# Moving a mixture-of-experts block's down product into the middle of the next block's gate and up product

## The reference, cut to what matters

```
def block_ffn(args):
    xb, e = args
    return (jax.nn.silu(xb @ w_gate[e]) * (xb @ w_up[e])) @ w_down[e]

yb = lax.map(block_ffn, (xin, blk_e)).reshape(NB * MOE_BLOCK, D)
y_assign = yb[dest] * sw[:, None]
routed = jax.ops.segment_sum(y_assign, stok, num_segments=T)
```

## Time and profile before

| what | value |
|---|---|
| time, median of 3 runs (lowest to highest) | 3617.73 us (3616.99 to 3620.08) |
| the profiled execution's own time | 3617.26 us |
| span of that execution in the trace | 3615.6 us |
| mean granted TensorE clock | 0.943 of full speed |
| TensorE matmul busy | 3229.3 us, 89% of the span |
| VectorE busy | 1567.9 us, 43% |
| ScalarE busy | 727.6 us, 20% |
| GpSimd busy | 728.1 us, 20% |
| first expert stage | about 1430 to 1789 us of the span |
| second expert stage | about 2560 to 3563 us of the span |

### The profile page before, as it was taken

How to read it: one execution, slowest core, us unless ns; L and a number is a source line. 1 busy time by engine, 2 the same in 40 slices (tenths; PEclk the granted TensorE clock), 3 DMA queues, 4 the chain that set the end, 5 groups by cost and what they waited for, 6 DMA issues and landing times. The chain is left out here.

```text
span 3615.6 us, 44557 instructions
## 1 busy us (share of the span) xinstructions
PE 3229.3 (89%) x14147; PEld 1611.6 (45%) x14148; DVE 1567.9 (43%) x2350; ACT 727.6 (20%) x1169; POOL 728.1 (20%) x932
## 2 busy tenths in 40 slices
PE   8999899978998995989688996999799999999992
PEld 4444355535664453333266773455333333333330
DVE  3332224446773123434346664334344444444444
ACT  2222223334552000111022220121011111111112
POOL 1000000000000000434410000000255555555552
PEclk9999999998999995999789998999899999999996
DMA  6110021123212215999530003101598999888876
GB/s 220 41 41 29 8 97 47 47 64 84 60 48 82 77 66 209 340 384 384 175 84 23 23 0 125 65 31 73 210 310 284 308 327 335 282 278 278 282 246 181
DMA packets 177201, 564.75 MB, mean 156 GB/s; under 512 B 18636, under 2 KB 88880, under 8 KB 139952
## 3 DMA queue, kind: packets, MB, share of 16 engines
q1 hardware_dynamic: 139456, 428.64, 31.3%
q0 software_dynamic: 35856, 133.74, 15.1%
q10 hardware_dynamic: 1800, 1.20, 0.1%
HBM read 460.27 MB, written 103.27 MB: 156 GB/s over the span
## 5 line engine op out<-in xcount | busy, mean ns | idle before, releaser
L1825 PE MATMUL gu_ps<-w_gu,second 128*64 x1680 | 755.4, 603 | 13.3 <-DVE h L1888 8.0
L1828 PE MATMUL gu_ps<-h,second 128*64 128x512 f32 x1680 | 755.4, 603 | 0.0
L1825 PEld LDWEIGHTS gu_ps<-w_gu,second 128*64 128x64 f32 x1680 | 224.3, 138 | 456.0 <-issue 444.2
L1753 POOL COPY idx<-moe_slot_tok 128x1 int32 (+1 forms) x109 | 21.9, 201 | 1782.4 <-POOLq L95 1739.8
L1851 PE MATMUL y_ps<-w_dn,hid_t 128*64 x824 | 375.6, 598 | 0.4 <-issue 0.2
L1854 PE MATMUL y_ps<-second,hid_t 128*64 128x512 f32 x824 | 375.7, 599 | 0.0
L352 PE MATMUL front<-second,wcol 128*128 128x512 f32 x768 | 330.4, 593 | 4.8 <-ACTq L63 2.4
L1888 DVE COPY h<-w_gu 128x4096 f32 x109 | 249.7, 2292 | 70.8 <-SPq L1705 70.5
L352 PEld LDWEIGHTS front<-second,wcol 128*128 128x128 f32 x768 | 145.9, 190 | 188.4 <-issue 188.4
L1773 POOL TENSOR_TENSOR idx_y<-moe_slot_tok,moe_side 128x1 int32<-128x1 int32 x103 | 123.2, 1196 | 520.4 <-ACT second L1874 520.4
L1828 PEld LDWEIGHTS gu_ps<-h,second 128*64 128x64 f32 x1680 | 224.3, 138 | 0.0
(11 more groups left out here) (435 smaller groups left out, 4902.6 us busy)
## 6 DMA issues: line engine op xcount, KB each, us to landing
w_gu<-in_w_gate_dram SPq DMA_DIRECT2D x96, 1024.0 KB, 13.2
w_gu<-in_w_up_dram SPq DMA_DIRECT2D x96, 1024.0 KB, 17.3
w_dn<-in_w_down_dram SPq DMA_DIRECT2D x96, 1024.0 KB, 10.5
wcol<-in_w_in_dram SPq DMA_DIRECT2D x12, 1024.0 KB, 5.3
qk_by_head<-stage SPq DMA_DIRECT2D x32, 384.0 KB, 3.3
qk<-qk_by_head SPq DMA_DIRECT2D x16, 768.0 KB
token_sums<-zero POOLq DMA_DIRECT2D x19, 512.0 KB, 12.7
token_sums<-second SPq DMA_DIRECT2D x16, 512.0 KB, 2.6
```

Source lines behind the costliest of these rows:

```text
L1825: nc.tensor.matmul(gu_ps[0:PART, slot], x_t[:, slot, c, 0:PART], w_gu[:, bass.ds(ws, 1), :, c, :].rearrange("p o g n -> p (o g) n"), start ...
L1828: last = nc.tensor.matmul(gu_ps[PART:P, slot], x_t[:, slot, c, PART:P], st_gu[:, slot, :, c, :], start=c == 0, stop=c == C - 1)
```

## The change

`finish(i, 1 - slot)`, the down product of block i - 1, no longer stands between the transposes of the next block's rows and those of the hidden rows. It is called inside the loop over the chunks of block i's gate and up product, ahead of the fifth of its eight chunks. On ScalarE, the copy of `y_ps` is written ahead of the SiLU of the same step. No instruction is added or removed; waits move with the work that they belong to.

```
@@ tensor, step @@
                 for c in range(C):
+                    if c == C // 2 and not first:
+                        finish(i, 1 - slot)
                     nc.tensor.matmul(gu_ps[0:PART, slot], x_t[:, slot, c, 0:PART],
...
                 last.then_inc(gu_ready, 1)

                 turn_rows(i + 1, 1 - slot, 16 if first else rounds + 32)
-                if not first:
-                    finish(i, 1 - slot)
                 pe.wait_ge(hid_ready, i + 1)
@@ scalar, step @@
             def step(i, slot, rounds):
-                a.wait_ge(gu_ready, i + 1)
-                s.activation(act_g[:, slot, :], gu_ps[:, slot, 0, :], ACT.Silu).then_inc(silu_done, 1)
                 if not (isinstance(i, int) and i == 0):
                     a.wait_ge(y_ready, 1 + i)
...
                     s.activation(y[:, 1 - slot, :], y_ps[:], ACT.Copy, scale=share[:, 1 - slot:2 - slot]).then_inc(y_taken, 1)
+                a.wait_ge(gu_ready, i + 1)
+                s.activation(act_g[:, slot, :], gu_ps[:, slot, 0, :], ACT.Silu).then_inc(silu_done, 1)
```

## The result

The changed kernel takes 3731.88 us (3730.98 to 3734.82, 4 runs) against 3618.09 us: a ratio of 1.0315, 95% interval 1.0297 to 1.0333. The profiled execution took 3731.26 us, 114.0 more than 3617.26. The forecast was 3686, with a range up to 3717. The direction and the place were right, the size was not.

The account below looks back on a forecast made before the run. TensorE's instruction list was taken to bound the second stage, and late weight transfers part of the first. Second stage +74.6 and first stage -5.8 gave +68.8 on 3617.26, so 3686 us, range 3674 to 3717.

Parts of the forecast that it names:

- the cover of VectorE's copy: Second stage: the down product fills TensorE while VectorE copies the transposed rows; uncovered, the copy costs 1.20 us a step.
- The row of step 0: First step of the second stage before, without down product: shows the copy uncovered; the new step is 13.17 us, 1.04 more.
- The first end: End of the first stage: the last result is taken earlier and the scatter follows, giving back 10.0 us.
- 9.74 us of step 0: Row transposes to next row transposes without a down product; plus 3.43 for its eight pairs gives a 13.17 us step.
- I take 0: Middle of the gate and up product: finish's number read, waits and slot number cost 0, within bounds 0 and 0.31 us.
- the 0.31 us: From copy end to first matmul in the first step: nearest price of unhidden stream work, upper bound a step for finish.
- a period over 13.4: Sign of being wrong: row transposes over 13.4 us apart would mean a gap or wait in the middle of the product.
- none is later: GpSimd's scatter and next gather, and the release of down-weight slots, come earlier in the step; no cost was added.
- The clock rival: Second stage: stalls lower TensorE's clock, 2.5 us lost every step, +198, about 3880 us; chance 0.04.
- The first stage: Its 24 steps mostly absorb the stalls in waits for late weights: +4.2 us, net -5.8 with the end's give-back.
- Not slower: Whole kernel: end effects and first-stage slack, 15.8 us, pay for the stalls; 3589 us at no wait; chance 0.03.
- the rival of the first stage paying in full: First stage: weight landings move with TensorE, so steps without waits pay, +24.2 us; 3706 us in all; chance 0.08.

Follow-up runs that it names:

- read_early: The changed kernel with the next step's expert number read into a register ahead of the row transposes; 3694.32 us, ratio 1.0210.
- silu_first: The changed kernel with the new order on TensorE alone, ScalarE keeping SiLU ahead of the result copy; 3702.58 us, ratio 1.0241.
- scatter_later: The changed kernel with GpSimd's scatter, and the gather after it, waiting until VectorE has copied the next rows; 3707.63 us, ratio 1.0245.
- four_steps_a_turn: The changed kernel with TensorE's loop holding four steps instead of two, so it jumps back half as often; 3723.86 us, ratio 1.0290.
- rows_in_middle_read_early: The changed kernel with row transposes also mid-product, ahead of the down product, and the next number read before the hidden-rows wait; 3823.14 us, ratio 1.0568.

## Why the prediction was wrong

**Right.** TensorE bounded the second stage, and the down product was the cover of VectorE's copy. The row of step 0 gave the price: 1.04 us a step, as read_early measures it in every step (13.17). The down product costs 3.43 us in its new place with no edge; its own read and waits cost nothing there (10.45 us in all undisturbed steps). The first end gave back 9.9 for 10.0; the second 7.7.

**The step that failed: 9.74 us of step 0 taken for every step.** The new step was set at 9.74 + 3.43, and the 9.74 holds 2.73 us from the row transposes to the product, as if only the copy led there. That TensorE's own way to the product, with the read of the expert's number at the start of every step and the jump back of the loop, would wait for nobody was put at nothing without a reason. The prediction looked at the number only where the change puts it, inside `finish` ("I take 0"), and there it was right. It took the 0.31 us from the end of the copy to the product as the nearest price of such work. But that row holds no read: in step 0 it had run while the copy was still to come (2588.45), in the kernel before:

```profile
L1819 PEldq TENSOR_LOAD <-moe_blk_e x1: 305/305/305, 2588.3 to 2588.3; - x1
```

The down product had covered this way as well as the copy. Once both are uncovered, the product starts behind the later of the two: the copy at 2.73 us, or start of the read + read + 0.8. Step 0 is written out, with no loop around it, and its read starts 1.0 us after the row transposes, so its own way ends at 1.0 + 0.3 + 0.8 = 2.1 us, 0.6 us under the copy. In the loop it is 1.32 + 0.30 + 0.83 = 2.45 us in one step and, behind the jump back, 1.71 + 0.30 + 0.83 = 2.84 in the next. With the slow reads of the change, 1.4 to 1.5 us, it is up to 4.0, as measured. In place of 79 steps of 13.17 us the runs showed a mean of 1074.8 / 79 = 13.61, and 13.17 with the read moved out (read_early). The prediction's own sign of being wrong, a period over 13.4, came, but not from the place that it named: the middle of the product stayed at 10.45, and the time was lost ahead of it. The trace of before had the read's duration, had I asked for that line (the same columns as above, of the kernel before):

```profile
L1819 PEldq TENSOR_LOAD <-moe_blk_e x105: 298/557/1040, 1436.0 to 3532.9; - x105
```

A read that takes up to 1.04 us where nothing waits for it was a bound of some 0.7 us a step more than I gave. The Trainium skill has a figure in DMA: Bandwidth & Descriptors, section Latency and other measured facts: about 600 ns as the floor of a `tensor_load`, without saying from which memory. The reads here, of a number in SBUF, go below it, 296 to 302 ns undisturbed, and far above it beside other traffic.

**The second part: "none is later".** I counted scatter and gather as harmless because they come earlier in the step. For a given block they do. But set against the row transposes, and so against the read, the scatter is issued 0.8 to 1.0 us ahead where it was 2.2, and the next gather 2.1 us behind where it was 0.75. The read was slow before too, with a median of 607 ns in the second stage, but covered. With the change it is 646, and up to 1488; with ScalarE's old order under the new order of TensorE, or with GpSimd held back, it is 302, and the times are 3731.9 against 3702.6 and 3707.6 us. Shown is that the read is slow when GpSimd's scatter and gather stand around the row transposes as they do here, and that the longest reads have the scatter's packets beside them. Why packets beside it make a read slow is open.

**The clock rival** was priced for every step and given 4 in 100. It came true in part: behind 6 of the 10 waits of 2.0 to 2.5 us, at some 1.6 us each (9.7 us). It was a consequence of the slow reads, and went with them (none in read_early, silu_first and scatter_later).

**The first stage** had 10.5 for 4.2; read_early has 7.0 there. So about half of the miss there (3.5 of 6.3) is the read, and the rest (2.8) was not followed.

**Not slower** and the rival of the first stage paying in full did not happen: that stage took 10.5 us more, not 24.2. VectorE's waits for weights there shrank as forecast, from 70.5 us to 36.3.

## What to carry to other kernels

Before work is moved away from a wait, list everything that it covers on the waiting engine: not only the other engine's result but also the engine's own scalar work (reads of a register, branches, address arithmetic), whose durations are in the trace although they count as no busy time. A step without the work, such as the first of a loop, gives a good floor but only one sample, and one without the loop's jump if it is written out; take the maximum of each uncovered duration from the whole trace as the upper bound. And moving one engine's work earlier moves the transfers behind it: ask what they then run beside.

## What the runs showed of the hardware that was not expected

- A register read of one number by TensorE's queue takes 296 to 302 ns undisturbed. It takes 0.95 us to 1.49 us in 20 steps of the change, all with packets of GpSimd's queue under way; in 19 of them they are the scatter's and began 0.1 to 0.6 us before the read. VectorE's read in `stage_down` became slow with the change too (300/305/330 ns before, 300/537/1447 after).
- In TensorE's loop the jump back holds a branch of 0.22 us, and the next step's read starts 1.71 us after the row transposes behind it and 1.32 without it.
- TensorE's products ran at half speed (granted clock 0.50) for three or four pairs behind 6 of the 10 waits of 2.0 to 2.5 us in the change. In four_steps_a_turn they did so 7 times, three of them behind waits of 1.6 to 1.7 us. With two waits of 0.9 us in each step of 14.08 us (rows_in_middle_read_early) every fourth step had such pairs and took 15.78; with one wait of 1.2 to 1.3 us in a step of 13.17 (read_early, second stage) none had.
- Two edges fewer between transposes and products in a step went with 12.13 - 11.78 = 0.35 us. The Trainium skill says in TensorEngine Tiling (Array Packing), section Key Properties, that changing the tiling mode drains TensorE, and these steps agree with it. No run changes the edges alone, so the 0.35 us is not shown to be theirs.
